# Reordering small products between dense groups in a two-layer hybrid encoder trunk: V products, the retention row, a late low split and the first norm's column sum

## What is computed

```python
h = rms_norm(x, norm_mix_g[l])
aq, ak, av, rq, rk, rv, rg, sz, sxbc, sdt = split(h @ w_in[l])
ya = swa_sink_attention(aq, ak, av, sinks, bias)     # 8 heads, 2 kv heads, window of 128
yr = retention(rq, rk, rv, rg, ret_gn_g[l])          # 4 heads, 64 x 128 state, group norm, silu(g) gate
ys = ssd_mixer(sz, sxbc, sdt, ...)                   # conv4 + silu, 8 heads, state 64, gated norm
x = x + concat(ya, yr, ys) @ w_out[l]
h = rms_norm(x, norm_ffn_g[l])
x = x + (silu(causal_dwconv(h @ w_up_a)) * (h @ w_up_b)) @ w_down[l]
```

## Time and profile before

| | us |
|---|---|
| median of three runs | 1261.06 |
| the profiled execution | 1259.85 |
| its span on the profile | 1258.0 |
| PE busy (matmul records) | 1249.1 (99%) |
| PE weight loads busy | 1017.9 (81%) |
| DVE, ACT, POOL busy | 659.4, 559.9, 585.6 |

### The profile page before, as it was taken

The page is one execution under the profiler, slowest core; times in us unless marked ns, Lnnn a source line. Parts: engine busy times, 40 slices in busy tenths (PEclk is TensorE's granted clock), DMA queues, the critical chain, the costliest instruction groups (busy, mean ns, idle before and its releaser), DMA issues.

```text
span 1258.0 us, 20786 instructions
## 1 busy us (share of the span) xinstructions
PE 1249.1 (99%) x6004; PEld 1017.9 (81%) x6004; DVE 659.4 (52%) x988; ACT 559.9 (45%) x896; POOL 585.6 (47%) x439
## 2 busy tenths in 40 slices
PE   8999999999999999999999999999999999999998
PEld 6888777888888888888878887788888888888886
DVE  7869875565554114432258799646655531234313
ACT  5542585464433224443336327854644432244434
POOL 4643433445444445554444434425454444455542
PEclk9999999999999999999999999999999999999999
DMA  7354232323333333333323633424233333455333
GB/s 221 104 159 117 70 80 81 103 74 116 100 96 96 97 96 93 98 92 100 94 77 89 186 89 84 100 61 109 76 111 98 100 94 98 117 125 125 101 100 127
DMA packets 121216, 130.68 MB, mean 104 GB/s; under 512 B 51226, under 2 KB 64058, under 8 KB 121148
## 3 DMA queue, kind: packets, MB, share of 16 engines
q1 hardware_dynamic: 120236, 128.32, 36.8%
q10 hardware_dynamic: 912, 1.49, 0.4%
HBM read 121.98 MB, written 2.56 MB: 99 GB/s over the span
## 4 chain that ended last, share of the span: by engine, by line
PE 75%; issue 13%; POOL 5%; ACT 4%; DVE 1%; DMA 1%; POOLq 0%; SPq 0%; ACTq 0%; DVEq 0%
PE dense L1276 69%; PE mix L1276 6%; POOL w_lo L481 5%; ACT w_hi L597 1%; DMA x<-in_xT 1%; ACT m_hi L614 0%; ACT L653 0%; ACT L702 0%; ACT L648 0%; POOLq L494 0%; ACT ssq L702 0%; POOL sq L513 0%; ACT L712 0%; DVE mx L1089 0%; DVE arena L1095 0%
## 5 line engine op out<-in xcount | busy, mean ns | idle before, releaser
L481 POOL TENSOR_TENSOR w_lo<-w_raw,w_hi 128x512 fp32r<-128x512 f32 x424 | 576.9, 1375 | 648.9 <-ACT w_hi L597 622.4
L1276 PE MATMUL dense<-h_hi,w_hi 128*128 128x512 f32 x992 | 389.6, 393 | 1.3 <-ACT w_hi L582 1.0
L1276 PE MATMUL dense<-h_lo,w_hi 128*128 128x512 f32 x992 | 386.3, 389 | 0.0
L597 ACT ACTIVATE w_hi<-w_raw 128x512 fp32r<-128x512 f32 x404 | 246.9, 626 | 277.8 <-PE dense L1276 257.4
L1276 PE MATMUL dense<-h_hi,w_lo 128*128 128x512 f32 x992 | 269.7, 390 | 0.0
L1276 PEld LDWEIGHTS dense<-h_hi,w_hi 128*128 128x128 f32 x992 | 186.2, 188 | 44.7 <-issue 4.8
L1276 PEld LDWEIGHTS dense<-h_hi,w_lo 128*128 128x128 f32 x992 | 186.1, 188 | 40.3 <-issue 1.7
L1276 PEld LDWEIGHTS dense<-h_lo,w_hi 128*128 128x128 f32 x992 | 186.4, 188 | 38.5 <-issue 0.5
L1276 PE MATMUL dense<-m_hi,w_hi 128*128 128x512 f32 x464 | 182.1, 392 | 0.4 <-DVE pad L961 0.4
L1276 PE MATMUL dense<-m_lo,w_hi 128*128 128x512 f32 x464 | 180.7, 389 | 0.0
L1276 PE MATMUL dense<-m_hi,w_lo 128*128 128x512 f32 x464 | 125.5, 389 | 0.0
(11 more groups left out here) (238 smaller groups left out, 1312.0 us busy)
## 6 DMA issues: line engine op xcount, KB each, us to landing
w_raw<-in_w SPq DMA_DIRECT2D x424, 256.0 KB, 2.6
arena<-cum_rows SPq DMA_DIRECT2D x8, 512.0 KB, 5.9
x<-in_xT SPq DMA_DIRECT2D x8, 256.0 KB, 7.5
arena<-arena SPq DMA_DIRECT2D x32, 64.0 KB, 2.2
arena<-arena SPq DMA_DIRECT2D x16, 128.0 KB, 2.9
out_y<-arena SPq DMA_DIRECT2D x7, 256.0 KB, 2.3
arena<-exp_rows SPq DMA_DIRECT2D x12, 128.0 KB, 6.4
w_raw<-in_w ACTq DMA_DIRECT2D x4, 256.0 KB, 6.3
```

The lines of the kernel that those rows point to most:

```text
L481: nc.gpsimd.tensor_tensor(w_lo[:, s, :], w_raw[:, s, :], w_hi[:, s, :].bitcast(f32), ALU.subtract).then_inc(lo_ready, 1)
L597: nc.scalar.activation(w_hi[:, slot, :], w_raw[:, slot, :], ACT.Copy).then_inc(hi_ready, 1)
L1276: return T.matmul(dst, lhsT, rhs, start=start, stop=stop)
```

## The change

- `DT` and `NORM` change places in the order.
- `NORM` no longer multiplies in plain fp32: ACT copies `ssq` to an fp32r high part in tile 10 of `m_hi`, DVE subtracts to get the low part in `m_lo`, and PE does two fp32r matmuls with the all-ones matrix.
- `AV0` moves from ahead of `QT0` to behind `D21`, ahead of `ZM0`.
- The second block's product with V is done by PE in a new step `AP2`, behind `SQ1`; ACT and DVE keep their parts where `AV2` stands.
- `SL` is cut in two: ACT's high parts are `SH`, DVE's low parts stay `SL`; `SH0 SL0` stand together, but `SL1` comes behind `D26`, so DVE empties D26's bank before it.
- `RA0` moves ahead of `AV3` and `D28`; all of the retention row, `RN RM` included, stands one dense unit earlier.
- SP issues the DMAs of q = 0, 1, 2 into `qkt` first, then a weight pack, then those of q = 3, then three packs.

```diff
-    "G0 G1 G2 G3 H0 H1 NORM DT L0 U0 DX L1 U1 L2 L3 TT TK ...
+    "G0 G1 G2 G3 H0 H1 DT NORM L0 U0 DX L1 U1 L2 L3 TT TK ...
-    ... D20 AX1 AV0 QT0 QT1 QT2 D21 ZM0 ZM1 AT1 AS2 SS0 AE2 ST0 D22 AX2 AV1 SQ0 SN0 ZM2 QT3 "
-    "D23 AT2 SX0 ZM3 SL0 AS3 SS1 AE3 D24 ST1 AX3 AV2 SN1 D25 SQ1 SX1 AC3 SL1 D26 AT3 D27 AV3 "
-    "D28 RA0 D29 RB0 RA1 D30 RQ0 RB1 RA2 D31 RQ1 RB2 RA3 D32 RQ2 RB3 D33 RQ3 D34 RN0 RM0 "
+    ... D20 AX1 QT0 QT1 QT2 D21 AV0 ZM0 ZM1 AT1 AS2 SS0 AE2 ST0 D22 AX2 AV1 SQ0 SN0 ZM2 QT3 "
+    "D23 AT2 SX0 ZM3 SH0 SL0 AS3 SS1 AE3 D24 ST1 AX3 AV2 SN1 D25 SQ1 AP2 SX1 AC3 SH1 D26 SL1 AT3 D27 RA0 AV3 "
+    "D28 RB0 RA1 D29 RQ0 RB1 RA2 D30 RQ1 RB2 RA3 D31 RQ2 RB3 D32 RQ3 D33 RN0 RM0 D34 "
...
+                def late_load(k):
+                    sp.wait_ge(lo_ready, QK_GROUP * SLOTS + (l * N_PACKS + SLOTS + k + 1))
+                    sp.dma_start(w_raw[:, k, :], a["w"][QK_GROUP * SLOTS + (l * N_PACKS + SLOTS + k)])\
+                        .then_inc(raw_loaded[k], 16)
...
                 for q in range(4):
-                    sp.wait_ge(lo_ready, QK_GROUP * SLOTS + (l * N_PACKS + SLOTS + q + 1))
-                    sp.dma_start(w_raw[:, q, :], a["w"][QK_GROUP * SLOTS + (l * N_PACKS + SLOTS + q)])\
-                        .then_inc(raw_loaded[q], 16)
+                    if q == 3:
+                        late_load(0)
                     for c in range(4):
                         sp.dma_start(qkt..., qkb...).then_inc(qkt_loaded, 16)
+                for k in range(1, SLOTS):
+                    late_load(k)
...
                     if step == "NORM":
+                        act.wait_ge(ssq_added, l * 14 + 7)
+                        nc.scalar.activation(m_hi[:, 10, :], ssq[:, :], ACT.Copy).then_inc(ssq_hi, 1)
                         act.wait_ge(m_ready[1], ready(name, 0, l))
                         nc.scalar.activation(rstd[:, :], M[1][:, :], ACT.Sqrt, scale=1.0 / D,
...
-                    elif step == "SL":
+                    elif step == "SH":
...
+                    if step == "NORM":
+                        dve.wait_ge(ssq_hi, l + 1)
+                        lo_from(m_lo[:, 10, :], ssq[:, :], m_hi[:, 10, :], ssq_lo)
...
                     elif step == "NORM":
-                        norm(l * 2, name, l)
+                        pe.wait_ge(c_loaded, 16 * N_CONST_LOADS)
+                        pe.wait_ge(ssq_lo, l + 1)
+                        take(name, 0, l)
+                        mm(M[1][:, :], ones_r[:, :], m_hi[:, 10, :], True, False)
+                        mm(M[1][:, :], ones_r[:, :], m_lo[:, 10, :], False, True).then_inc(m_ready[1], 1)
...
-                    elif step == "AV":
+                    elif step == "AP" or step == "AV" and n != 2:
+                        name = f"AV{n}"
```

More of the change, by code:

```diff
@@ L307, in build @@
         pool_sq_ready = sem("pool_sq_ready")
+        ssq_hi, ssq_lo = sem("ssq_high"), sem("ssq_low")
         dchain, achain = sem("vector_chain"), sem("scalar_chain")
@@ L920, in _ @@
                     step, n = step_of(name)
-                    if step == "U":
+                    if step == "NORM":
+                        dve.wait_ge(ssq_hi, l + 1)
+                        lo_from(m_lo[:, 10, :], ssq[:, :], m_hi[:, 10, :], ssq_lo)
+                    elif step == "U":
                         if n == 0:
```

## The result

The changed kernel takes 1269.82 us (median of eight runs, 1265.39 to 1273.27) against 1261.85 us for the kernel before, run beside it (eight runs, 1260.87 to 1262.40): a ratio of 1.0063, 95% interval 1.0044 to 1.0082. It is slower, as forecast, but by 8.0 us where 3.7 was forecast, and it lies above the range, which ended at 1267.2. Its runs also spread over 8 us where those of before spread over 1.5.

A forecast was written before the change was run, and what follows sets the result against it. TensorE, with matmul records over 99% of the span, was taken as the bound. The terms 1.55 + 0.8 - 0.5 gave 1.85 us a layer, 3.7 in all, so 1264.8 us from 1261.06, range 1261.0 to 1267.2.

The forecast's parts named there:

- TT: PE's step reading DX's result: starts later because the square root now waits for DT, +1.55 us a layer.
- The rival in which TT doesn't wait: Before TT: rstd is not on PE's path, PE keeps its 0.5 us, -0.2 us a layer, 1260.7; chance 0.12.
- PE's own saving: At NORM: two fp32r matmuls take 0.45 us instead of 0.95 in plain fp32, so PE saves 0.5 us.
- The step that failed: Before TT: PE's saved 0.5 us becomes part of a 2.0 us wait, counted as +1.55 us a layer.
- AV2's product behind SQ1: PE waits about 1 us for SQ1's low part from DVE, so D26 starts later: +0.8 us a layer.
- the rival in which SQ1 doesn't wait: At SQ1: low part comes 1 us earlier while TT still waits, +1.05 us a layer, 1263.2; chance 0.10.
- AV0 and the ZM products: Behind D21: ZM products need 1.3 us instead of 2.37, clear of POOL's low part; chain to SQ1 keeps its time.
- the rival in which it slips: Chain to SQ1: ZM products stay at 2.37 us, everything behind 0.9 us later a layer, 1266.6; chance 0.14.
- AV3 with RA0, D28: From AV3 to RB0: D28's wait goes and two small groups become one, 7.75 to 7.23 us, -0.5 us a layer.
- The retention row: RN and RM come one unit earlier with the same distance to RB3: no effect on time.
- Sum: Whole kernel: 1.55 + 0.8 - 0.5 = 1.85 us a layer, 3.7 us in all, median 1264.8 us; chance 0.59.
- that case: Lower end of the range: TT does not wait, -0.2 us a layer, 1260.7; chance 0.12.

The follow-up runs named there:

- e1: Changed kernel with eight idle fp32r matmuls filling PE's wait before TT: 1266.25 us, ratio 1.0040.
- e4: Kernel before with only DT and NORM exchanged, the norm product staying plain fp32: 1268.73 us, ratio 1.0062.
- e10: Changed kernel with NORM, in its fp32r form, back ahead of DT: 1262.32 us, ratio 1.0008.
- e5: Changed kernel with the norm's order, product and semaphores as before, and AP2 ahead of SQ1: 1260.80 us, ratio 1.0000.
- e9: e7 with ACT making the high parts of packs 14 and 15 ahead of unit 2's silu: 1265.51 us, ratio 1.0031.
- e7: Changed kernel with reciprocal and DX ahead of U0, packs 8 to 11 ahead of U0's silu, AP2 ahead of SQ1, RX and RL one unit earlier: 1261.03 us.
- e8: e5 with RN and RM back behind D34, as before the change: 1260.75 us, ratio 0.9998.
- e2: Kernel before with only the norm part: DT ahead of NORM, norm product by fp32r high and low parts: 1267.22 us, ratio 1.0044.
- e12: e7 with ACT making pack 14's high part alone, right behind unit 2's silu: 1259.80 us, ratio 0.9991.

## Why the prediction was right or wrong

**TT.** Right, to 0.02 us: forecast +1.55, measured 1.57 (e1's stage, and 11.80 against 10.24 us from the first small-product matmul to TT in the second layer). The wait of 2.0 us, its releaser and both layers are as written, and e4 and e10 separate its cause: the order alone makes it, the new product in the old order doesn't. The rival in which TT doesn't wait has fallen. Smaller than written was PE's own saving: DT and NORM take 2.42 us together, where NORM and DT took 2.80, so 0.4 and not 0.5; it made no difference, since it went into the wait.

**The step that failed** is the one that turned this wait into time. The text put "the 0.5 us that PE saved becomes part of a wait of 2.0 us" at the length of the wait and no more; neither the sum nor a rival had a term for the work behind it, done at the lower clock. What the runs showed in its place is the granted clock at half behind the wait; it cost 3.27 us in the first layer of the profiled execution and 1.7 in the second. By execution that term is 0 to 8 us: after's two full-clock runs are at 1265.4 and 1265.7, its two lowest clocks (0.993) at 1273.0 and 1273.3. For the median it is 1269.82 - 1266.25 = 3.6 us, the difference to e1, or 3.0 against the kernels before beside each. The profile could have warned: in the kernel before the granted clock was low until 4.9 us, so clock is given and taken in this kernel, and a wait of 2 us ahead of D4 had no counterpart in it, since PE's longest wait past the first 10 us was 0.2 us. A new wait longer than any that the trace shows should have had a bound above its own length.

**AV2's product behind SQ1.** Right: forecast a wait of about 1 us and +0.8 a layer; 0.85 us of wait, D24 to D26 +0.85, +0.73 counted from D5. e5 takes the wait away. The rival in which SQ1 doesn't wait has fallen.

**AV0 and the ZM products.** Right: 1.28 us for two, between two instructions of GpSimd, so the chain to SQ1 kept its time and the rival in which it slips has fallen. The Trainium skill, page "SBUF — State Buffer", section "Who interferes with whom", on which that rival was weighed, is borne out here (1.28 us alone, 2.37 beside a low part), by the RX instructions ahead of D42 and by line 999 of e9. Lines 994 and 997 of e9 have one tensor operand and are not what the sentence in the prediction speaks of.

**AV3 with RA0, D28.** Right: forecast -0.5, measured -0.46 up to D35.

**The retention row.** "RN and RM come one unit earlier with the same distance to RB3: nothing" was wrong by 0.40 us a layer. RX and RL kept their place while RN and RM went ahead. So RX0 starts 3.53 us behind D35's start instead of 4.36, the next ones meet GpSimd's low parts otherwise than before, and ACT comes 0.46 us late to D42's pack. What was looked at was the distance to RB3, not what GpSimd does beside RX. e7 and e8 remove the wait in two ways, 0.40 in the stages each; in the time that is too little to be shown.

**Sum.** Full clock: 1.57 + 0.73 - 0.46 + 0.40 = 2.24 a layer, 4.5 us (forecast 3.7), which from 1261.3 gives 1265.8; e1 measured 1266.25. The forecast's direction and its mechanisms held; its median missed by 5.0 us: 3.6 are the clock and 0.8 D42's wait, and the 0.6 left is within what the base moved (1261.06 to 1261.85). The range, built from mechanisms that all act at full clock, could not hold it. (Its lower end is given as 1261.0; the sum for that case is 1260.7.)

What stays open: why the same wait brought the fall in six of eight runs of after and not in the two others, in both layers of e2's profile and in neither of e4's, and in the first layer of e9 and not in the second. No experiment was made on this.

## What to carry to other kernels

Where TensorE is busy 99% of the time, cost a new wait twice: its length, and the work behind it at half clock. Here 1.2 us was free of the second and 2.0 us was not; filling the wait with idle matmuls gives a test of it in one run. A step exchanged with its neighbour in a hand-written order costs nothing to write and must be followed to the end of every chain that hangs on it: the exchange of DT and NORM carries nearly all of this change's loss. And making operands earlier isn't free where GpSimd's work on them then falls beside VectorE's instructions: two packs too early cost 4.5 us (e9 against e7), one in the right gap gained 1.0 in the stages (e12 against e7).

## What the runs showed of the hardware beyond what was expected

- Behind PE's wait of 1.95 us with the four small products after it, the granted clock was at half from 36.44 to 43.27 us and, in the second layer of the same execution, from 664.49 to 667.90. In e2 it was at half from 35.24 to 42.06 and from 663.29 to 666.70. Behind waits of 0.85 and 1.2 us it stayed up in every profile; behind 1.95 us (e4, both layers) and 2.66 us (e9's second layer) it stayed up as well. So a wait of this length is a risk with a price that varies, not a fixed cost.
- VectorE's instruction of 32 columns in 128 partitions took 0.17 us alone and 1.16 to 1.27 beside a low part of GpSimd, also in forms with one tensor operand (lines 994 and 997 of e9). The excess, 1.0 to 1.1 us, is that of the 512-column RX instructions (0.78 to 1.79). The reciprocal of 32 columns (line 998) took 0.35 us in e9 and 0.36 in e7.
